# Output products of three attention mixers made of three rounded products instead of one float32 product

## The reference, cut to what matters

```python
def stick_breaking_attention(x, w_qkv, w_o):
    ...
    o = merge_blocks(lax.map(block, jnp.arange(s // Q_BLOCK)))
    return from_heads(o) @ w_o          # [256, 1024] @ [1024, 1024]

for i in range(DEPTH):                  # DEPTH = 4, three kinds in turn
    h = h + 0.5 * swiglu(rms_norm(h, norm_ffn1[i]), ...)
    h = h + mix                         # mix = attention(rms_norm(h), ...)
    h = h + 0.5 * swiglu(rms_norm(h, norm_ffn2[i]), ...)
```

## Time and profile before

| | |
|---|---|
| median of 3 runs (lowest, highest) | 3934.51 us (3933.24, 3935.13) |
| the profiled execution | 3947.08 us, span 3945.3 us |
| mean granted TensorE clock | 0.884 |
| float32 products L793, all phases | x288 records of 144 matmuls, 128 of them in the four mixers that change |
| head stages | about 278 to 351, 798 to 865, 1301 to 1367 and 1811 to 1884 us |

### The profile page before, as it was taken

One profiled execution on the slowest core, in us unless ns is written; L12 is line 12 of the kernel. 1 busy time (PEld: TensorE's weight loads), 2 busy tenths in 40 slices (PEclk: granted clock), 3 DMA queues, 4 the chain that ended last, 5 costly groups with the idle time before them and its releaser, 6 DMA issues.

```text
span 3945.3 us, 40806 instructions
## 1 busy us (share of the span) xinstructions
PE 2997.9 (76%) x14576; PEld 2222.6 (56%) x14576; DVE 2711.0 (69%) x4748; ACT 1232.7 (31%) x1807; POOL 1054.5 (27%) x1133
## 2 busy tenths in 40 slices
PE   8999999989999999999999944433338964433334
PEld 7897888968886688887886721111114661111111
DVE  6655676666765667664764677778775487778786
ACT  5444444344442444444442311111111231111110
POOL 2000000000000000000000266666663056666665
PEclk9999999999999999999999967776679987666668
DMA  6634555435554445561563399999998279999998
GB/s 211 211 115 145 192 195 185 175 113 187 183 187 144 136 160 197 190 225 61 183 206 119 137 351 350 360 360 363 366 365 316 77 270 360 356 361 366 363 368 331
DMA packets 411558, 940.73 MB, mean 238 GB/s; under 512 B 24656, under 2 KB 207472, under 8 KB 411392
## 3 DMA queue, kind: packets, MB, share of 16 engines
q0 software_dynamic: 150800, 547.19, 36.9%
q1 hardware_dynamic: 259744, 390.09, 29.2%
q10 hardware_dynamic: 848, 1.31, 0.1%
HBM read 937.45 MB, written 1.05 MB: 238 GB/s over the span
## 4 chain that ended last, share of the span: by engine, by line
PE 54%; DVE 30%; issue 5%; another core or an unknown queue 4%; DMA 3%; POOL 2%; ACT 1%; DVEq 0%; SPq 0%; POOLq 0%; ACTq 0%
DVE wide_ring L2411 11%; PE pair L930 7%; PE pair L937 7%; DVE pair L2451 7%; PE pair L699 5%; PE pair L701 5%; PE pair L700 5%; PE pair L772 4%; PE pair L935 4%; PE pair L932 4%; PE pair L793 4%; DVE deep_ring L2411 3%; DMA wide_ring<-in_ffn_w_gate_up 2%; PE pair L780 1%
## 5 line engine op out<-in xcount | busy, mean ns | idle before, releaser
L1327 PE MATMUL pair<-wide_ring,arena 128*128 128x512 f32 x816 | 444.2, 693 | 664.6 <-issue 459.4
L1691 DVE TENSOR_TENSOR wide_lo<-wide_ring,wide_hi 128x2048 fp32r<-128x2048 f32 x228 | 522.3, 2291 | 401.5 <-ACT wide_hi L1410 396.2
L1327 PEld LDWEIGHTS pair<-wide_ring,arena 128*128 128x128 f32 x816 | 171.7, 221 | 935.4 <-issue 846.2
L2563 POOL TENSOR_TENSOR small<-small,minus_half 128x2 f32<-128x2 f32 (+2 forms) x29 | 25.2, 870 | 2346.2 <-DVE small L1841 1694.0
L1410 ACT ACTIVATE wide_hi<-wide_ring 128x2048 fp32r<-128x2048 f32 x228 | 434.6, 1911 | 479.8 <-DMA wide_ring<-in_ffn_w_gate_up 313.7
L930 PE MATMUL pair<-x_both,wide_hi 128*128 128x512 f32 x1344 | 532.8, 396 | 2.8 <-DVE wide_lo L1691 2.5
L937 PE MATMUL pair<-x_both,wide_hi 128*128 128x512 f32 x1344 | 531.7, 396 | 0.0
L2411 DVE CUSTOM_DVE_ANT_0 wide_ring<-wide_ring,pair 128x1024 f32<-128x1024 f32 x408 | 490.4, 1209 | 22.5 <-issue 22.2
L2584 POOL DMA_INDIRECT wide_ring<-in_peer_v,pk_idx x408 | 392.7, 962 | 244.1 <-issue 112.7
L2584 POOL DMA_INDIRECT wide_ring<-in_peer_u,pk_idx x408 | 393.0, 963 | 165.5 <-issue 92.0
L935 PE MATMUL pair<-x_both,wide_lo 128*128 128x256 f32 x1344 | 374.2, 278 | 0.0
(11 more groups left out here) (349 smaller groups left out, 5825.1 us busy)
## 6 DMA issues: line engine op xcount, KB each, us to landing
wide_ring<-in_ffn_w_gate_up SPq DMA_DIRECT2D x176, 1024.0 KB, 9.5
deep_ring<-in_ffn_w_down SPq DMA_DIRECT2D x88, 1024.0 KB, 5.0
wide_ring<-in_sb_w_qkv SPq DMA_DIRECT2D x12, 2048.0 KB, 12.5
wide_ring<-in_w_in SPq DMA_DIRECT2D x12, 2048.0 KB, 9.6
wide_ring<-in_peer_w_q SPq DMA_DIRECT2D x8, 2048.0 KB, 14.0
wide_ring<-in_moba_w_qkv SPq DMA_DIRECT2D x6, 2048.0 KB, 12.3
deep_ring<-in_sb_w_o SPq DMA_DIRECT2D x8, 1024.0 KB, 7.6
deep_ring<-in_w_out SPq DMA_DIRECT2D x8, 1024.0 KB, 7.6
```

Source lines behind the costliest of these rows:

```text
L1327: ins = mm(acc[t][h][:, :], pk_diag[:, s % 2, k], row_at(ph, row)[:, h * 512:(h + 1) * 512], start=first, stop=last, skip_group_check=True)
L1691: V.tensor_tensor(wide_lo[:, split_at(ph, j)], half_panel(ph, wide_ring[:, slot], j), wide_hi[:, split_at(ph, j)].bitcast(F32), ALU.subtra ...
```

## The change

For the kinds in `SPLIT_OUT` each float32 matmul of `deep_piece` becomes a `split_mm` of three fp32r matmuls, and the wait for the panel's load becomes a wait for its low part. ScalarE makes the high part of each out panel in `out_high`, VectorE the low part in `out_low`, in place in the ring; `mixed_out` makes a high and a low part of the mixed values of a head, the second behind the first.

```diff
@@ TensorE, deep_piece
+                if ph.kind in SPLIT_OUT:
+                    pe.wait_ge(S["deep_lo"], ph.at["deep_lo"] + k + 1)
+                else:
+                    await_deep(ph, k)
...
+                    if ph.kind in SPLIT_OUT:
+                        ins = split_mm(acc[t][h][:, :],
+                                       [x[:, t * P:(t + 1) * P] for x in lhs(c)],
+                                       [x[:, c, h * 512:(h + 1) * 512] for x in (out_hi[k % 2], deep_ring_lo[:, out_slot(ph, k)])],
+                                       k == 0 and c == 0, last and c == 1)
+                        continue
@@ ScalarE, stick_breaking (at the end of a pass) and softmax_heads (the same, other passes)
+                    if i in (4, 8, 12, 16):
+                        out_high(ph, i // 4 - 1)
...
+            def out_high(ph, k):
+                act.wait_ge(deep_in[out_slot(ph, k)], 16 * ((ph.at["deep"] + k) // DSLOTS + 1))
+                act.wait_ge(S["deep"], ph.at["deep"] + max(k - 1, 0))
+                A_(out_hi[k % 2][:], deep_ring[:, out_slot(ph, k)], ACT.Copy).then_inc(S["deep_hi"], 1)
...
+                    if i in (3, 7, 12, 17):
+                        out_high(ph, (3, 7, 12, 17).index(i))
@@ VectorE
+            def out_low(ph, k):
+                dve.wait_ge(S["deep_hi"], ph.at["deep_hi"] + k + 1)
+                slot = out_slot(ph, k)
+                V.tensor_tensor(deep_ring_lo[:, slot], deep_ring[:, slot], out_hi[k % 2][:].bitcast(F32),
+                                   ALU.subtract).then_inc(S["deep_lo"], 1)
...
             def mixed_out(ph, h, o):
...
-                V.tensor_copy(o[p0:p0 + HD, h // 2], work[3][p0:p0 + HD, (h % 2) * TOK:(h % 2 + 1) * TOK]
-                              ).then_inc(S["mixed_read"], 1)
+                hi, lo = (x[p0:p0 + HD, h // 2] for x in o)
+                both = work[3][p0:p0 + HD, (h % 2) * TOK:(h % 2 + 1) * TOK]
+                chain(V.tensor_copy(hi, both))
+                V.tensor_tensor(lo, both, hi.bitcast(F32), ALU.subtract).then_inc(S["mixed_read"], 1)
...
+                    if i in (5, 9, 13, 16):
+                        out_low(ph, (5, 9, 13, 16).index(i))
@@ VectorE, softmax_heads
+                    if i in (3, 7, 13, 17):
+                        out_low(ph, (3, 7, 13, 17).index(i))
```

More of the change, by code:

```diff
@@ L65 @@
 ADDS = (*MIXERS, "ffn")
+SPLIT_OUT = ("sb", "moba", "mla")
 BY_TILE = [(0, 0), (0, 1), (1, 0), (1, 1)]
@@ L170 @@
                 wide_lo=2 * FFN_STEPS, deep_hi=FFN_STEPS + 1, deep_lo=FFN_STEPS + 1),
-    "sb": dict(wide_hi=12, wide_lo=12, wide=12, wide_read=12, deep=4, deep_parts=3, resid=4, scale_mm=1, scores=HEADS, masked=HEADS, log1p=HEADS,
+    "sb": dict(wide_hi=12, wide_lo=12, wide=12, wide_read=12, deep=4, deep_hi=4, deep_lo=4, deep_parts=3, resid=4, scale_mm=1, scores=HEADS, masked=HEADS, log1p=HEADS,
                softplus=HEADS, tail=HEADS, tail_read=HEADS, weights=HEADS, mixed=HEADS,
                mixed_read=HEADS),
-    "moba": dict(wide_hi=12, wide_lo=12, wide=12, wide_read=12, deep=4, deep_parts=3, resid=4, rotated=1, turned=8, moved_even=4,
+    "moba": dict(wide_hi=12, wide_lo=12, wide=12, wide_read=12, deep=4, deep_hi=4, deep_lo=4, deep_parts=3, resid=4, rotated=1, turned=8, moved_even=4,
                  moved_odd=4, scores=HEADS, masked=HEADS, row_max=HEADS, exps=HEADS,
                  probs=HEADS, probs_T=HEADS, weights=HEADS, mixed=HEADS, mixed_read=HEADS),
-    "mla": dict(wide=18, wide_read=18, deep=4, deep_parts=3, resid=4, rotated=3, mean_square=2, rstd=2,
+    "mla": dict(wide=18, wide_read=18, deep=4, deep_hi=4, deep_lo=4, deep_parts=3, resid=4, rotated=3, mean_square=2, rstd=2,
                 turned=20, moved_even=10, moved_odd=10,
@@ L221, in build, with rounded_view @@
         wide_ring = sb("wide_ring", [P, GSLOTS, KT, GCOLS])
+        with ExitStack() as rounded:
+            def rounded_view(name, shape):
+                return rounded.enter_context(nc.sbuf_tensor(name, shape, F32R))
+            deep_ring_lo = rounded_view("deep_ring_lo", [P, DSLOTS, DROWS // P, D])
+            rounded_view("beside_resid", [P, TT, D])
+            out_hi = [rounded_view(f"out_hi_{k}", [P, DROWS // P, D]) for k in range(2)]
         deep_ring = sb("deep_ring", [P, DSLOTS, DROWS // P, D])
@@ L270, in build @@
         sb_v = cut(4096, TT, D)
-        oT = cut(10240, KT, TOK)
+        mixed_hi = wide_lo[:, 0].rearrange("p k u m -> p (k u m)").rearrange("p (c t) -> p c t", c=KT)
+        sb_mixed = (mixed_hi, x_both[:, 4:8].rearrange("p k a t -> p (k a) t"))
+        soft_mixed = (mixed_hi, deep_hi[:].rearrange("p c n -> p (c n)").rearrange("p (c t) -> p c t", c=KT))
         mo_qk = cut(0, TT, 2 * D)
         mo_T = cut(6144, 2 * KT, TOK)
-        mo_oT = cut(10240, KT, TOK)
         mo_v = cut(4096, TT, D)
@@ L282, in build @@
         ml_c = cut(16384, TT, MLA_IN)
-        ml_oT = cut(10240, KT, TOK)
         ml_cT = xT[:, 0:5, :]
@@ L529, in turn_bank, with out_slot @@
             return (first + g) % 4
+        def out_slot(ph, k):
+            return (ph.at.get("deep", 0) + k) % DSLOTS
         def split_turn_bank(ph, n):
@@ L788, in deep_piece @@
             def deep_piece(ph, k, last, lhs, t, h):
-                await_deep(ph, k)
-                w = deep_ring[:, (ph.at.get("deep", 0) + k) % DSLOTS]
-                for c in range(2):
+                if ph.kind in SPLIT_OUT:
+                    pe.wait_ge(S["deep_lo"], ph.at["deep_lo"] + k + 1)
+                else:
+                    await_deep(ph, k)
+                w = deep_ring[:, out_slot(ph, k)]
+                for c in range(2):
+                    if ph.kind in SPLIT_OUT:
[4 more added lines that the diff above has]
+                        continue
                     ins = mm(acc[t][h][:, :], lhs(c)[:, t * P:(t + 1) * P],
@@ L980, in out_product @@
             def out_product(ph, k, src):
-                deep_product(ph, k, k == 3, lambda c: src[:, 2 * k + c, :])
+                deep_product(ph, k, k == 3, lambda c: [x[:, 2 * k + c, :] for x in src])
             def stick_breaking(ph):
@@ L1020, in stick_breaking @@
                         pe.wait_ge(S["mixed_read"], seen(at.get("mixed_read", 0) + i - 3))
-                        out_product(ph, (i - 7) // 4, oT)
+                        out_product(ph, (i - 7) // 4, sb_mixed)
             def mix_values(ph, h, v, w):
@@ L1066, in softmax_heads @@
                             pe.wait_ge(S["mixed_read"], seen(ph.at.get("mixed_read", 0) + i - 3))
-                        deep_piece(ph, k, False, lambda c: o[:, 2 * k + c, :], piece // 2, piece % 2)
+                        deep_piece(ph, k, False, lambda c: [x[:, 2 * k + c, :] for x in o], piece // 2, piece % 2)
                     if 0 <= i - 2 < HEADS:
@@ L1085, in qk @@
                     return mo_T[p0:p0 + HD, c], mo_T[p0:p0 + HD, KT + c]
-                softmax_heads(ph, qk, mo_v, mo_oT)
+                softmax_heads(ph, qk, mo_v, soft_mixed)
             def latent_attention(ph):
@@ L1129, in qk @@
                     return ml_T[0:MLA_QK, h, 0:TOK], ml_T[0:MLA_QK, h, TOK:2 * TOK]
-                softmax_heads(ph, qk, ml_v, ml_oT)
+                softmax_heads(ph, qk, ml_v, soft_mixed)
             def parallel_mixer(ph):
@@ L1991, in stick_breaking @@
                     if 0 <= i - 3 < HEADS:
-                        mixed_out(ph, i - 3, oT)
+                        mixed_out(ph, i - 3, sb_mixed)
+                    if i in (5, 9, 13, 16):
+                        out_low(ph, (5, 9, 13, 16).index(i))
                 add_deep(ph, 4, None)
@@ L2045, in block_attention @@
                 move_turned(dve, ph, range(8), move, "moved_odd")
-                softmax_heads(ph, HD ** -0.5, mo_oT)
+                softmax_heads(ph, HD ** -0.5, soft_mixed)
             def latent_attention(ph):
@@ L2122, in latent_attention @@
                 move_turned(dve, ph, range(16, 20), move, "moved_odd")
-                softmax_heads(ph, MLA_QK ** -0.5, ml_oT)
+                softmax_heads(ph, MLA_QK ** -0.5, soft_mixed)
             def parallel_mixer(ph):
```

## The result

The changed kernel took 3970.28 us (median of 4, 3967.46 to 3973.14), the kernel before, measured beside it, 3934.82: ratio 1.0096, 95% interval 1.0083 to 1.0108, so +35.5 us. The forecast was 3969 (3944 to 3998), slower.

A forecast was written before the change was run, and what follows sets the result against it. Per four stick-breaking heads, VectorE and TensorE were both nearly full for 9 us, then TensorE alone for 6.9. Queue and chain +25 us (TensorE's saving included) and clock +10 on the 3934.5 us median gave 3969 us (3944 to 3998).

The forecast's parts named there:

- TensorE's term: Four head stages: three fp32r matmuls replace each float32 one, 1.4 us less on 12 panels, 0.35 on four; -18.2 us.
- E: Rival: f32r matmuls run no faster in this place, +18 us on the sum, 3987 us; chance 0.02.
- Three for four passes: Output products: a float32 product taken as four array passes would make a panel 5.15 us, the whole saving 27.5 us.
- Low parts in the queue: Stick breaking: low parts in VectorE's queue ahead of masks delay them; +7.1 us a stage, +14 for two.
- queue and chain: Four head stages: delays from queue order and dependent steps, without the clock; 14 + 5 + 6 = +25 us.
- Block and latent attention: Low parts delay masks and pieces where VectorE is full; +5.0 us in block attention, +6 in latent attention.
- The clock, +10: TensorE's granted clock falls to half after new waits; four stage ends at 2.5 us each, nothing elsewhere; +10 us.
- (a): VectorE, `mixed_out`: a low-part subtraction of 0.42 us for each head's mixed values, +1.7 us per four heads.
- (b): VectorE, `out_low`: a low part of 2.29 us for each of 16 out panels, 2.2 us to the next start.
- Rival C: VectorE's low parts run in its own waits, only TensorE's saving of -18.2 us is left: 3916 us; chance 0.05.
- Rival D: Low parts hidden in block and latent attention (-4.6 us each), stick breaking pays 14: +5, 3939 us; chance 0.08.

The follow-up runs named there:

- kernel kept busy: Changed kernel with short matmuls to an unread bank put into TensorE's waits; +28.5 us against the kernel before, +31.1 when run again.
- products alone: Changed kernel without mixed values' low parts, panels' low parts cut to 64 columns, one full high part a stage; -15.0 us against the kernel before.
- placed kernel: Changed kernel, same arithmetic, panels' high and low parts moved in the queues to idle times, some low parts in halves; +1.3 us against the kernel before.
- short low parts: Changed kernel with the panels' low parts cut to 64 columns, in their place in VectorE's queue; -0.9 us against the kernel before.

## Why the prediction came out right

**TensorE's term, -18.2 us: right.** Measured by itself -15.0 in the time, -20.3 in the stages, of which (30.7 - 20.5)/3 = 3.4 are clock, so -16.9. At equal half clock a stick-breaking stage gives 4.4 us (60.0 against 64.4) and the latent one 4.3 (53.8 against 58.1), where the forecast has 4.55 for each stage. The period's 1.40 is exact, and product 0 of the changed kernel starts at 298.90 and hands over to the next scores at 304.57, 5.67 us for 24 matmuls with the start. E falls. Three for four passes would have made it 27.5; the measured price of a matmul kept the sum right. (The prediction has product 0 from 297.35 to 304.22 where the earlier trace rows have 297.19 and 304.15; the 0.43 us is right all the same, the starts of its 16 records being 0.429 us apart.)

**Low parts in the queue: right in stick breaking.** Forecast and measured: mask 8 to 12 17.0 and 17.04; mask 10 at 7.1 and 7.08; subtraction 8 at 8.0 and 8.01; out_low(3) 3.0 behind subtraction 14 and 2.95, subtraction 15 5.2 and 5.27. The last product stands 9.35 us behind subtraction 14 instead of 4.52, +4.8 where about 4 was forecast. The stage: 7.1 for queue and chain and part of the clock's 10, measured +7.3 and +7.7. The clock's share follows from its places: the changed kernel's two stages pay 0.7 and 1.3 us ahead of mask 8 (25.4 and 26.0 us behind mask 0, 24.7 at full clock in the kernel kept busy) and 2.0 and 1.6 at the end, the kernel before 2.6 and 2.5 at its start (mask 8 at 26.1 and 26.0, where 22.1 of the products alone at full clock and their 1.4 make 23.5). That is +0.1 and +0.4. Queue and chain are 7.3 in both stages, 0.2 over the forecast.

**Block and latent attention: right in the mechanism, short in size.** Forecast against measured, from the first mask: piece 0 2.9 and 3.7, piece 8 4.4 and 5.9, last product 5.3 and 7.0; latent attention's piece 0 3.9 and 4.9. The forecast laid the instructions out at full clock. The trace has a further stretch at half clock 14 to 21 us behind the first masks, where I had put it at the ends alone; the two stages spend 17.1 and 20.5 us so, 10.2 and 6.8 before. Stages: 5 and 6 forecast, +8.0 and +10.7 measured, less 6.8/3 = 2.3 and 13.7/3 = 4.6 of clock: 5.7 and 6.1. These two rest on the third holding there.

**The clock, +10: the cost is there, by another way, and near in size by luck.** I had priced four ends at 2.5 us each and nothing else. The ends hold 20.5 us at half clock, which cost 2.0 and 1.6 in stick breaking and, at a third, 1.1 in each of the others; the softmax stages have 13.7 more elsewhere, which is 4.6; and the starts of stick breaking have 6.8 less, which gives back 3.1. Net 7.4, or 9 if each of the 27.3 us more at half clock is taken at a third.

So: queue and chain 7.3 + 7.3 + 5.7 + 6.1, about 26 against 25, clock 7 against 10, stages +33.6. The rest to +35.5 is beside the stages, and no run says where from. The three partly cancel, so the hit to 1 us is in part luck; the sign and the main term are not.

**Which part was the dear one.** The prediction gave no split between its (a) and (b). Left out alone, the mixed values' low parts give back 11 us and the panels' 38, for 27 and 33 us of work; without clock, at a third, some 8 and 25. The rest of the new work lay in waits, most of the mixed values' in stick breaking. Rival C's condition ("no mask on the path starts later") is nearly what the placed kernel fulfils in stick breaking, where the stages are 4.3 and 5.0 us under the kernel before, 2.5 at equal clock; C had 4.55. Rival D supposed that 4.4 us of VectorE's short waits would hold 3.9 us in the softmax stages; with short low parts these stages drop by 10.0 and 11.7 us, by 6.6 and 7.1 without clock at a third, for 8.3 us less work in each, so the waits had held little of it.

## What to carry to other kernels

- Added work on an engine that is not the bound costs most of its length if it stands in that engine's queue ahead of something the bound waits for: making 16 subtractions of 2.28 us short gave back 38 us between the heads, some 25 without the clock; left whole and moved, in the main to where the engine waited for a product or a projection, the stages were as short (242.0 us) as with the short ones (241.8). Read where the engine's long waits are, and move the work there before deciding on the change.
- The clock is part of the price: waits put into TensorE's schedule cost again where it falls to half, here about a third of a us for each us at half clock, and the gain of a move can be larger than the work moved for the same reason. Compare stages only beside their half clock: two executions of the changed kernel differ by 2.7 us in the sum of the stages.
- Look at each place of use: once placed, the change paid in stick breaking, not in the softmax stages.

## What the runs showed of the hardware

- GpSimd's 128x2048 subtraction took 4.51 us, VectorE's 2.28; beside it VectorE's operations between SBUF operands ended with GpSimd's or up to 0.4 us behind it (0.29 us became 3.03 and 4.29, a 0.55 one 3.48); a mask and a subtraction out of PSUM, reductions and a reciprocal did not.
- The same kernel, whole, took 3970 and 3833 us in two measurements. The traces agree to 2 us up to the fourth head stage (1838.90 and 1840.59 us); the expert rows behind it were gathered at 355 to 384 GB/s in most slices of the one and at 409 in the other. Slices 1 to 40 of the span, GB/s, first run and second:

```profile
GB/s 210 209 115 139 186 183 183 194 112 160 196 188 145 99 173 205 180 214 66 165 186 190 91 318 369 365 361 355 369 384 302 76 283 362 356 371 360 369 371 327
```

```profile
GB/s 217 190 145 116 183 185 198 225 36 190 182 186 203 75 149 187 181 198 203 77 171 209 123 123 386 409 409 409 409 409 356 171 139 391 409 409 409 409 409 333
```

Why, no run here shows; without the kernel before measured beside it no kernel above could be compared.
